# A gated differential-attention and Fourier encoder layer on eight cores: an unnormalised difference of the two attention maps, rope on raw projections, the first weight matrix kept in bf16, conversions spread, and new costs in the planner

## The reference, cut to what matters

```
SEQ = 2048; D_MODEL = 1024; N_HEADS = 8; HEAD_DIM = 64; EPS = 1e-6     # 24 sequences in all
h = rmsnorm(x, g_mix)
q, k, v, f = split(h @ w_in)                     # 1024 + 1024 + 1024 + 512 columns
q = rope(rmsnorm(q per 64-wide map, g_q)); k = rope(rmsnorm(k per 64-wide map, g_k))
p = softmax(q k^T / 8) for two maps of each head
a = p[:, :, 0] - lam * p[:, :, 1]                # differential attention map
o = rmsnorm(a @ v, g_sub) * (1 - lambda_init)    # per head, width 128
attn_out = o @ w_attn_br
four_out = real(fft2(f per group of 128)) @ w_four_br
gates = sigmoid(h @ w_gate + b_gate)
x = x + (gates[0] * attn_out + gates[1] * four_out) @ w_out
h2 = rmsnorm(x, g_mlp)
y = x + square(relu(h2 @ w_up)) @ w_down
```

## Time and profile before

| | |
|---|---|
| Time, median of 3 runs | 4775.1 us (4769.97 to 4881.26) |
| The profiled execution | 4777.7 us, span of its slowest core 4776.2 us |
| Spans of the eight cores | 4735.9 to 4776.2 us |
| Busy share: PE, DVE, ACT, POOL | 84%, 60%, 54%, 1% |
| Transfers | 893.82 MB, mean 187 GB/s |
| Chain that ended last | PE 56%, DMA 22%, issue 11%, ACT 6%, DVE 4% |

### The profile page before, as it was taken

The page is one execution under the profiler, slowest core; times in us unless marked ns, Lnnn a source line. Parts: engine busy times, 40 slices in busy tenths (PEclk is TensorE's granted clock), DMA queues, the critical chain, the costliest instruction groups (busy, mean ns, idle before and its releaser), DMA issues.

```text
span 4776.2 us, 54033 instructions; the slowest of 8 cores (4735.9 to 4776.2 us)
## 1 busy us (share of the span) xinstructions
PE 4017.4 (84%) x19092; PEld 1857.9 (39%) x19092; DVE 2854.1 (60%) x4195; ACT 2565.2 (54%) x5114; POOL 40.5 (1%) x50
## 2 busy tenths in 40 slices
PE   3675665879899899898986778899898989889899
PEld 1232222334444444454432334444453434334344
DVE  4776466887766766776717887766774133232331
ACT  3354464567877777787714567877782121211211
POOL 0000000000000000000000000000000000000000
PEclk9998787989999999999999999999999999999999
DMA  9789999878888889888869678878876355455452
GB/s 208 177 159 150 169 205 200 149 150 228 207 184 205 209 183 213 212 196 205 198 153 228 144 170 207 215 178 221 214 179 220 138 199 196 165 194 191 162 198 106
DMA packets 1253117, 893.82 MB, mean 187 GB/s; under 512 B 1020016, under 2 KB 1173104, under 8 KB 1212400
## 3 DMA queue, kind: packets, MB, share of 16 engines
q1 hardware_dynamic: 1205520, 842.13, 69.6%
q0 software_dynamic: 47328, 48.24, 7.4%
HBM read 590.33 MB, written 122.68 MB: 149 GB/s over the span
## 4 chain that ended last, share of the span: by engine, by line
PE 56%; DMA 22%; issue 11%; ACT 6%; DVE 4%; SPq 0%; POOL 0%; ACTq 0%; DVEq 0%; POOLq 0%
PE pall L380 56%; DMA sb_aT<-sb_p 16%; ACT sb_p L391 3%; DMA sb_wr<-sb_wr 3%; DVE sb_wr L397 2%; ACT sb_wr L391 2%; DMA sb_wr<-w_in 1%; DMA sb_wr<-gbc 1%; DVE sb_p L400 1%; DMA sb_wr<-x 1%; DVE sb_wr L400 0%; SPq L413 0%; ACT sb_sm L391 0%; ACT sb_ors L391 0%; DVE sb_sm L581 0%
## 5 line engine op out<-in xcount | busy, mean ns | idle before, releaser
L380 PE MATMUL pall<-sb_wr 128*128 128x512 bf16 x12672 | 3048.6, 386 | 375.4 <-DMA sb_wr<-sb_wr 189.9
L380 PEld LDWEIGHTS pall<-sb_wr 128*128 128x128 bf16 x12672 | 1244.6, 99 | 1957.8 <-issue 285.6
L391 ACT ACTIVATE sb_p<-pall 128x1024 bf16<-128x1024 f32 x1536 | 1565.2, 1028 | 594.8 <-PE pall L380 317.9
L380 PE MATMUL pall<-sb_kb,sb_qz 128*128 128x512 bf16 x3072 | 938.2, 394 | 176.9 <-ACT sb_p L391 173.0
L397 DVE TENSOR_TENSOR sb_wr<-sb_wr 128x256 f32<-128x256 f32 (+3 forms) x1254 | 640.3, 523 | 450.7 <-ACT sb_wr L391 367.3
L400 DVE SCALAR_TENSOR_TENSOR sb_p<-sb_p,sb_sm 128x2048 bf16<-128x2048 bf16 x384 | 901.4, 2348 | 8.1
L391 ACT ACTIVATE sb_wr<-pall 128x512 bf16<-128x512 f32 (+1 forms) x744 | 443.4, 598 | 562.2 <-PE pall L380 556.1
L397 DVE TENSOR_TENSOR sb_wr<-pall,sb_wr 128x512 f32<-128x512 f32 (+1 forms) x480 | 325.6, 688 | 510.4 <-PE pall L380 465.8
L380 PE MATMUL pall<-sb_aT,sb_vb 128*128 128x256 bf16 x3072 | 416.5, 295 | 187.9 <-DMA sb_aT<-sb_p 187.6
L380 PEld LDWEIGHTS pall<-sb_kb,sb_qz 128*128 128x128 bf16 x3072 | 279.5, 100 | 585.6 <-ACT sb_p L391 389.1
L380 PEld LDWEIGHTS pall<-sb_aT,sb_vb 128*128 128x128 bf16 x3072 | 316.9, 105 | 308.4 <-DMA sb_aT<-sb_p 227.1
(11 more groups left out here) (35 smaller groups left out, 545.4 us busy)
## 6 DMA issues: line engine op xcount, KB each, us to landing
sb_wr<-wb_up SPq DMA_DIRECT2D x96, 1024.0 KB, 5.9
sb_wr<-wb_down SPq DMA_DIRECT2D x96, 1024.0 KB, 5.4
sb_wr<-wb_gate SPq DMA_DIRECT2D x48, 1024.0 KB, 7.1
sb_wr<-x SPq DMA_DIRECT2D x48, 512.0 KB, 5.6
sb_vb<-v SPq DMA_DIRECT2D x48, 512.0 KB, 4.5
sb_kb<-k SPq DMA_DIRECT2D x48, 512.0 KB, 5.3
sb_wr<-wb_attn SPq DMA_DIRECT2D x24, 1024.0 KB, 8.6
sb_wr<-x SPq DMA_DIRECT2D x12, 2048.0 KB, 11.0
```

What stands on the lines that cost most here:

```text
L380: P.op("pe", lambda e: e.matmul(out, lhsT=lhsT, rhs=rhs, start=start, stop=stop), reads, writes, dur=max(0.08, (n / 2.4 + 4) / 960.0))
L391: r_ = P.op("act", lambda e: e.activation(out=out, in_=in_, func=func, **kw), reads, writes, dur=(n + 205) / 1200.0 + (0.1 if accum_out is ...
```

## The change

- Stage C: the two maps are no longer divided by their row sums. With the sums s0 and s1 of the exponentials p0 and p1, DVE now makes the factor c = -lam s0 / s1, scales map 1 by it, and adds it to map 0 with a plain addition of bf16 (was: both scaled, the second by a scalar-tensor-tensor operation). The row is then s0 times what it was. The output norm would cancel that factor but for its epsilon, so epsilon is multiplied by s0 squared: DVE makes a diagonal tile `dg` of s0 squared (one more operation a query tile), and four matmuls of 128 columns per output norm add epsilon times it to the mean square in bank 7. The square goes into `oout` and no longer into a buffer of its own.
- Stage A: the rope products are taken of the raw projection in PSUM, the sign-and-half swap in one operation (a reversed view), their sum moves to POOL, and the reciprocal root is multiplied in last. Temporaries t1 and t2 have two buffers each.
- w_in: A0 loads it with the cast as before, but its loads past the first wait for given transposes of normed tiles, and each block is stored as bf16 to `wb_in` from SP's queue. A1 and A2 load the bf16 blocks from SP's queue.
- Conversions: of a head's four, two are issued at its first and two at its fifth query tile. The calls in stage A of sequence 1 come behind these in the program, when the 8 x 4 places of C(0,0) have already used up all 25.
- Start: constants, tables and gains (`setup`) are set up after the second norm tile, and the tables' scratch lies in weight slots 3 and 4 rather than in `hT`.
- Planner: accumulator exponentials cost 0.1 us more, transposes of n tiles 0.6 + 0.012 n us and 9290 n bytes, an addition on POOL 1.2 us.
- The stage order is now a string.

```
+ORDER = "A0 C00 A1 D00 D01 C01 D02 D03 C10 A2 D10 D11 C11 D12 D13 C20 D20 D21 C21 D22 D23"
+CONV = (2, 2, 1, 1)
...
-                      dur=(n + 205) / 1200.0 + (0.1 if accum_out is not None else 0.0), table=tb)
+                      dur=(n + 205) / 1200.0 + (0.2 if accum_out is not None else 0.0), table=tb)
...
-                         nbytes=-tiles * 5100, dur=0.1 + tiles * 0.019)
+                         nbytes=-tiles * 9290, dur=0.6 + tiles * 0.012)
...
             for t in range(NT):
-                norm_tile(t)
+                marks.append(norm_tile(t))
+                if s == 0 and t == 1:
+                    setup()
...
+            def wload_in(j, after=()):
+                if s > 0:
+                    return wload(wb_in[j].rearrange("p (k n) -> p k n", k=8), 8, [("wbin", j)], nslot=5)
+                b = wload(w_in_r[:, :, j * 512:(j + 1) * 512], 8, [], q="pool", nslot=5, after=after)
+                DMA("sp", wb_in[j], wvb(b * SL, SL), ("wis", j % 2), wvc(b * SL, SL), [("wbin", j)], 1 << 20)
+                return b
...
+                        TT(t1.rearrange("p (m d) -> p m d", m=8), zn.rearrange("p (m d) -> p m d", m=8), cg, ALU.mult, [bres(bk)] + wvc(A_RT[ri], 512), ct1, 512)
+                        z4 = zn.rearrange("p (m h d) -> p m h d", m=8, h=2)[:, :, ::-1, :]
+                        sg = rt[:, kk + 1, :].rearrange("p (h d) -> p h d", h=2).unsqueeze(1).to_broadcast([128, 8, 2, 32])
+                        TT(t2.rearrange("p (m h d) -> p m h d", m=8, h=2), z4, sg, ALU.mult, [bres(bk)] + wvc(A_RT[ri], 512), ct2, 512)
+                        TT(t1, t1, t2, ALU.add, ct1 + ct2, ct1, 512, eng="pool")
                         rstd_small(sm[:, so + 16:so + 24], sm[:, so:so + 8], [("ssq", wi)], ("q", wi), 1.0 / 64, 8)
...
+                        TT(wvb(A_QK[wi], 512).rearrange("p (m d) -> p m d", m=8), t1.rearrange("p (m d) -> p m d", m=8), rb, ALU.mult,
+                           ct1 + [("smr", ("q", wi))], wvc(A_QK[wi], 512), 512)
...
-                    if s == 0 and half == 0 and qt == 0:
-                        convert(4, [x_])
+                    if s == 0 and half == 0 and qt % 4 == 0:
+                        convert(CONV[qt // 4], [x_])
...
-                    P.op("dve", lambda e, P1=P1, sc=sc: e.tensor_scalar(out=P1[:], in0=P1[:], scalar1=sm[:, sc + 7:sc + 8], scalar2=neglam,
-                                                                       op0=ALU.mult, op1=ALU.mult), rp1 + [("r2", r), ("neglam",)], rp1, dur=0.75)
-                    STT(P0[:], P0[:], sm[:, sc + 6:sc + 7], P1[:], ALU.mult, ALU.add, rp0 + rp1 + [("r2", r)], rp0, 2048)
+                    P.op("dve", lambda e, P1=P1, sc=sc: e.tensor_scalar_mul(out=P1[:], in0=P1[:], scalar1=sm[:, sc + 7:sc + 8]),
+                         rp1 + [("c2", r)], rp1, dur=0.8)
+                    TT(P0[:], P0[:], P1[:], ALU.add, rp0 + rp1, rp0, 2048, fast=2)
+                    g2 = gn[0] % 2
+                    P.op("dve", lambda e, sc=sc, g2=g2, qi=qt % 4: e.tensor_scalar(out=dg[g2][:, qi, :], in0=ident, scalar1=sm[:, sc + 4:sc + 5], scalar2=sm[:, sc + 4:sc + 5],
+                                                                                 op0=ALU.mult, op1=ALU.mult), [("s2", r), ("cmat",)], [("dg", g2, qt % 4)], dur=0.2)
...
+                        ACT(oout[oi][:], osb[:], AF.Square, [("osb",)], [("oout", oi)], 512)
+                        MM(bank(7), onesm, oout[oi][:], True, False, [("oout", oi), ("cmat",)], [bres(7)])
+                        for qi in range(4):
+                            MM(pall[:, 7, qi * 128:(qi + 1) * 128], epsm[:], dg[oi][:, qi, :], False, qi == 3, [("dg", oi, qi), ("epsm",)], [bres(7)], n=128)
+                        ACT(ors[:], bank(7), AF.Ln, [bres(7)], [("ors",)], 512)
```

More of the change, by code:

```diff
@@ L354, in build_program @@
         aT = [sb("aT%d" % i, [128, 2, SEQ], BF16) for i in range(3)]
+        epsm = sb("epsm", [128, 128], BF16)
+        dg = [sb("dg%d" % i, [128, 4, 128], BF16) for i in range(2)]
         osb = sb("osb", [128, 512], F32)
-        osq = sb("osq", [128, 512], BF16)
         ors = sb("ors", [128, 512], F32)
@@ L359, in build_program @@
         wr = sb("wr", [128, WN], BF16)
-        onesm, ccm, nscm = [cmat[:, i, :] for i in range(3)]
+        onesm, ccm, nscm, ident = [cmat[:, i, :] for i in range(4)]
         bg, gsub = vecs[:, 0:16], vecs[:, 16:17]
@@ L396, in TT @@
         def TT(out, in0, in1, op, reads, writes, n, fast=1, eng="dve"):
-            return P.op(eng, lambda e: e.tensor_tensor(out=out, in0=in0, in1=in1, op=op), reads, writes, dur=(n / fast + 150) / 960.0)
+            return P.op(eng, lambda e: e.tensor_tensor(out=out, in0=in0, in1=in1, op=op), reads, writes,
+                        dur=1.2 if eng == "pool" else (n / fast + 150) / 960.0)
         def STT(out, in0, scalar, in1, op0, op1, reads, writes, n):
@@ L457, in build_program @@
         assert D_RL[1] + 512 <= WN
[L459 to L477, removed]
@@ L567, in stage_a @@
                 for nm, c0 in (("k", 1024 + ps * 512), ("q", ps * 512), ("v", 2048 + ps * 512)):
-                    bw[nm] = wload(w_in_r[:, :, c0:c0 + 512], 8, [], q="pool", nslot=5)
+                    bw[nm] = wload_in(c0 // 512, (marks[4 + nq[nm]],) if ps else ((marks[nq[nm]],) if nm != "k" else ()))
                 for t in range(NT):
@@ L582, in stage_a @@
                              wvc(A_SQ, 1024), [("ssq", wi)], dur=0.69)
+                        kk = 2 if nm == "k" else 0
+                        t1, t2 = wvf(A_T1[wi], 1024), wvf(A_T2[wi], 1024)
+                        ct1, ct2 = wvc(A_T1[wi], 1024), wvc(A_T2[wi], 1024)
+                        zn = bank(bk)
+                        cg = rt[:, kk, :].unsqueeze(1).to_broadcast([128, 8, 64])
+                        TT(t1.rearrange("p (m d) -> p m d", m=8), zn.rearrange("p (m d) -> p m d", m=8), cg, ALU.mult, [bres(bk)] + wvc(A_RT[ri], 512), ct1, 512)
@@ L593, in stage_a @@
-                        zv = zn.rearrange("p (m d) -> p m d", m=8)
-                        t2v = wvf(A_T2, 1024).rearrange("p (m d) -> p m d", m=8)
-                        for hf in range(2):
-                            sg = rt[:, kk + 1, hf * 32:(hf + 1) * 32].unsqueeze(1).to_broadcast([128, 8, 32])
-                            TT(t2v[:, :, hf * 32:(hf + 1) * 32], zv[:, :, (1 - hf) * 32:(2 - hf) * 32], sg, ALU.mult,
-                               czn + wvc(A_RT[ri], 512), wvc(A_T2, 1024), 256)
@@ L610, in stage_a @@
                     vs = wvb(vo, 2048).rearrange("p (h t d) -> p h t d", h=4, t=4)
-                    CP(vs[:, :, tl, :], bank(bk).rearrange("p (h d) -> p h d", h=4), [bres(bk)], wvc(vo, 2048), 512, eng="act")
+                    x_ = CP(vs[:, :, tl, :], bank(bk).rearrange("p (h d) -> p h d", h=4), [bres(bk)], wvc(vo, 2048), 512, eng="act")
+                    if s == 1:
+                        convert(CONV[2 + ps], [x_])
                     if tl == 3:
@@ L831, in stage_d @@
             DMA("sp", y_d[r0:r0 + 512, :].rearrange("(t p) d -> p t d", p=128), x1v, "yst", wvc(D_X1, 8192), [("y", s, c)], 1 << 21)
-        stage_a(0)
-        for s in range(nseq):
-            for half in range(2):
-                stage_c(s, half)
-                if half == 0 and s + 1 < nseq:
-                    stage_a(s + 1)
-                for c in (half * 2, half * 2 + 1):
-                    stage_d(s, c)
+        for tok in ORDER.split():
+            f = {"A": stage_a, "C": stage_c, "D": stage_d}[tok[0]]
+            f(*[int(x) for x in tok[1:]])
         yres = [("y", s, tc) for s in range(nseq) for tc in range(NTC)]
```

75 lines of the change are left out of this document (44 added, 31 removed).

## The result

The changed kernel takes 0.9546 of the time of the kernel before (95% interval 0.9512 to 0.958). With the kernel before at 4772.5 us (the median of its four runs) that is 4556 us, 217 us less; the changed kernel's six runs lay between 4546 and 5125 us. In some runs of every kernel one die or both show a lower clock and the time is longer by up to a tenth or more, so the ratios here are of the other runs. The profiled execution has a span of 4566.3 us, 210 us less than that of before.

What follows compares the result with a forecast made beforehand. PE was taken to bound D, late inputs to idle PE in attention, DVE to pace stage A, DMA to nearly fill the first 1000 us. Terms 20 + 85 + 25 + 20 + 60 - 35 = 175 gave 4600 us; range 4470 to 4730.

Steps and rivals of the forecast that it cites:

- likeliest case: Whole kernel: the forecast's own range, 4540 to 4660 us, given 0.45.
- D's tail: From 3600 us only stage D runs, held by PE at 163 us per stage; the change saves nothing there.
- Order and planner: Attention beside D: a third of PE's 188 us of waits goes, 60 us, bounds 0 and 150.
- Rope: Stage A: less DVE time per product, 85 us (A2 40, A0 and A1 25 and 20), bounds 40 and 140.
- period of 2.7 us: Stage A2: time between groups of eight matmuls falls to about 2.7 us from 3.47.
- Feeding: Loads, conversions and start: w_in 25 us, conversions 20 us, start 20 us.
- Maps and epsilon: Attention: DVE's saving of 290 us nearly all hidden; epsilon matmuls cost PE 35 us, bounds 20 and 60.
- shorter chain: Attention: 1.0 us less latency between last exponential and transpose, counted inside the order's term.
- stand-still: Rival: the first 1000 us, held by DMA at 0.93, don't move; 4700 us; chance 0.19 for 4660 to 4740.
- The order was worth most of its bound: Rival: PE's 188 us of waits mostly go, 150 + 25 us; time 4460; chance 0.24 for 4430 to 4540.
- POOL did not hold up stage A: Rival: POOL's addition holds up stage A; at 5 us each, near 4980 us; chance 0.02.
- The planned order: Rival: dearer transposes make the planner's order worse, 4780 to 4850 us; slower through POOL or order 0.05.

Runs made afterwards that it cites:

- b_maps: Kernel before with only the unnormalised difference of maps and its epsilon in the output norm: ratio 1.0018, 4781 us.
- b_rope: Kernel before with only rope on raw projections, its addition on POOL, the root last and two buffers: ratio 0.9880, 4715 us.
- b_plan: Kernel before with only the planner's new numbers for accumulator exponentials and for transposes: ratio 0.9759, 4658 us.
- a_dveadd: Changed kernel with the sum of the rope products on DVE instead of POOL: ratio 0.9582, 4573 us.

## Why the prediction was right, and where its terms were off

The forecast was 4600 us, 175 us less; 217 were measured, which is 4556 us, inside the range of 4470 to 4730 and inside the likeliest case's own 4540 to 4660, near its fast end. By its terms:

- **What bounds the kernel.** D's tail was read rightly. That DVE is hidden in attention is borne out by b_maps, but for up to some 40 us that the epsilon matmuls could cover. That DVE paces stage A is borne out by b_rope's 57 us; the shorter pause of A2 is no proof of it, since the planner's numbers shorten it as well. But I looked for it mainly in A2, and most of rope's gain came before 1000 us, beside a DMA share of 0.97.
- **Order and planner: 60 forecast, 115 measured.** This is the term that was mis-sized. I let a third of PE's 188 us of waits in the overlapped stretches go. Of the two waits, that for `aT` fell by two thirds (46.6 to 13.0 us between 1000 and 2200) and that for exponentials by a tenth. The steps also counted only these stretches; over the span PE's wait for `aT` fell from 188 to 96 us in b_plan, and 34 us of that lay before 1000 us (87.9 to 53.6). What I tied to both numbers belongs for the most part to the transposes' numbers. In the changed kernel the wait before 1000 us is back at 92.9.
- **Rope: 85 forecast (40 in A2, 25 and 20 in A0 and A1), 57 measured**, within its bounds of 40 to 140, but about 40 of it before 1000 us and about 20 in A2. The period of 2.7 us was not found: the row-by-row pattern of A2 is gone. Longer blocks of matmuls have mostly taken its place, with a few groups of eight about 3 us apart, and they wait for ACT as well as DVE.
- **Feeding: 65 forecast (25 + 20 + 20), 44 measured.** Inside it the conversions were under-sized (20, measured 43 by undoing them in the changed kernel, between 4 and 82), which would leave about nothing for start and w_in. Those two were not tried alone. For the start the trace says it by itself: 20 us were forecast, and although the first matmul comes 34 us earlier, as many matmuls are done by 100 us as before. The mechanism was right, a bank held until the tables are back, but it lasts to 62 us and not to 50 or 55, and the second block of w_in was at 45.
- **Maps and epsilon: -35 forecast with the shorter chain booked elsewhere; about -9 to +11 measured together.** The 37 us of PE were not seen in the time. Whether the 1 us shorter chain pays for them isn't settled: the two were not tried apart.
- **The rivals.** The first 1000 us moved, by some 60 us of work, so their stand-still is refuted. The order was worth most of its bound, 115 of 150, though the time of 4460 was not reached. POOL did not hold up stage A; the estimate of 1.1 to 1.3 us per addition fits its median of 1.271 us, not its mean of 1.418, which the additions that meet DVE's operations draw up. The planned order was not worse.

That 175 came so near 217 is in part luck, since the errors went opposite ways: the order 55 too low, rope 28 and feeding 21 too high, and maps and epsilon charged with some 26 us that they didn't cost. With the order's term right, the sum would have been 230.

## What to carry to other kernels

In a kernel whose queues are ordered by a simulated plan, look first at the planned cost of the transfers that PE waits for. Here planning a transpose at 3.3 us of the DMA pipe instead of 1.8 (and 0.4 us less on SP) brought 2%, while 290 us less of DVE work, with 37 us more of PE, brought nothing, and five other numbers made truer brought nothing either. Before a busy engine is relieved, ask in which stage it ends a wait last. In this kernel bulk transfers that share the pipe with transposes were better issued in small groups, although the pipe was nearly full. And an earlier first instruction is no gain by itself: count the work done by a later time.

## What the runs showed of the hardware

- POOL adds 512 f32 elements per partition in 1.418 us (median 1.271, longest 3.449), DVE in 0.683.
- While POOL adds, DVE slows down, and only in some operations. In the changed kernel's trace the 16 of 384 bf16 additions of 2048 elements that lie beside a POOL addition take 1.741 us on average, the others 1.223. The f32 to bf16 product of 128x512 takes 0.924 beside one (58 of 192) and 0.684 otherwise; over all 0.757, and 0.684 in a_dveadd. The rope products with one operand in PSUM take 0.680 and 0.687, so they aren't slowed. The Trainium skill (GPSIMD Engine Reference, specifications) says that POOL's SBUF interfaces are shared with VectorE and contended by operations of VectorE with two SBUF inputs or in a two-port mode; these rows agree.
- The bf16 addition of 2048 elements at 1.222 us in a_dveadd agrees with the 1224 ns of the Trainium skill (VectorE: DVE Perf Modes, the perf-mode tier table).
- A one-column operation with two per-partition scalars takes 0.268 us, and a 128x128 bf16 one 0.326 us (0.300 without POOL's additions), against 0.162 for the reciprocal of one column.
